# Mixture of experts in float32: gate and up in column blocks of 1024, 1024, 1024, 512 in place of seven of 512

## The reference

```python
def _moe(h, w_router, w_gate, w_up, w_down):       # 8 experts, 2 of them for each token
    ...
    xs = xf[tok_sorted]
    hid = jax.nn.silu(lax.ragged_dot(xs, w_gate, group_sizes)) * lax.ragged_dot(xs, w_up, group_sizes)
    ys = lax.ragged_dot(hid, w_down, group_sizes)
    ys = ys * gates.reshape(-1)[order][:, None].astype(ys.dtype)
    out = jnp.zeros_like(xf).at[tok_sorted].add(ys)
```

## Time and profile before

| | |
|---|---|
| time, median of 3 runs | 2108.22 us (2107.17 to 2116.1) |
| span of the profiled execution | 2110.6 us; nothing of it lies outside the core's span |
| PE busy | 1991.3 us, 94% |
| DVE busy | 1566.7 us, 74% |
| ACT busy | 1266.8 us, 60% |
| moved by DMA | 504.07 MB, 239 GB/s over the span |

### The profile page before, as it was taken

One profiled execution on the slowest core, in us unless ns is written; L12 is line 12 of the kernel. 1 busy time (PEld: TensorE's weight loads), 2 busy tenths in 40 slices (PEclk: granted clock), 3 DMA queues, 4 the chain that ended last, 5 costly groups with the idle time before them and its releaser, 6 DMA issues.

```text
span 2110.6 us, 27963 instructions
## 1 busy us (share of the span) xinstructions
PE 1991.3 (94%) x10196; PEld 1664.4 (79%) x10196; DVE 1566.7 (74%) x1654; ACT 1266.8 (60%) x1469; POOL 373.2 (18%) x165
## 2 busy tenths in 40 slices
PE   6999789999998999988879999999999999999997
PEld 5787678998766899876668878788887888878885
DVE  3336656665677666668769989898998989889896
ACT  3535234433642434465248778787887878788785
POOL 4478463000640300164020000000000000000000
PEclk9899899999999999999989999999999999999999
DMA  8343334555431555542159989899998989999994
GB/s 245 100 160 130 108 112 161 198 181 180 135 96 67 161 193 185 180 126 90 51 199 366 375 319 374 322 371 331 358 377 315 375 321 371 368 323 374 330 365 161
DMA packets 244789, 504.07 MB, mean 239 GB/s; under 512 B 10448, under 2 KB 59216, under 8 KB 244576
## 3 DMA queue, kind: packets, MB, share of 16 engines
q1 hardware_dynamic: 241968, 499.02, 67.0%
q0 software_dynamic: 976, 2.25, 0.5%
q10 hardware_dynamic: 1760, 1.64, 0.2%
HBM read 501.83 MB, written 1.05 MB: 238 GB/s over the span
## 4 chain that ended last, share of the span: by engine, by line
PE 84%; DVE 9%; ACT 3%; issue 2%; DMA 1%; POOL 1%; DVEq 0%; SPq 0%; ACTq 0%
PE bank L565 25%; PE bank L567 24%; PE bank L566 24%; DVE arena L1475 2%; PE bank L994 1%; PE bank L1062 1%; PE bank L1020 1%; DMA arena<-in_w_in 1%; DVE arena L1471 1%; PE bank L626 1%; PE bank L868 1%; POOL w_lo_sb L549 1%; PE bank L763 1%; ACT w_hi_sb L1156 1%; DVE arena L1825 1%
## 5 line engine op out<-in xcount | busy, mean ns | idle before, releaser
L1514 DVE TENSOR_TENSOR w_lo_sb<-arena,w_hi_sb 128x1024 fp32r<-128x1024 f32 x672 | 803.0, 1222 | 92.1 <-ACT w_hi_sb L1136 68.1
L1136 ACT ACTIVATE w_hi_sb<-arena 128x1024 fp32r<-128x1024 f32 x672 | 709.8, 1061 | 185.3 <-PE bank L567 185.3
L565 PE MATMUL bank<-w_hi_sb,left_hi_sb 128*128 128x512 f32 (+1 forms) x1472 | 585.9, 398 | 26.7 <-POOL w_lo_sb L549 9.2
L566 PE MATMUL bank<-w_lo_sb,left_hi_sb 128*128 128x512 f32 (+1 forms) x1472 | 573.0, 389 | 0.0
L567 PE MATMUL bank<-w_hi_sb,left_lo_sb 128*128 128x512 f32 (+1 forms) x1472 | 572.9, 389 | 0.0
L1156 ACT ACTIVATE w_hi_sb<-arena 128x1024 fp32r<-128x1024 f32 (+1 forms) x269 | 279.3, 1051 | 405.9 <-PE bank L567 347.5
L549 POOL TENSOR_TENSOR w_lo_sb<-arena,w_hi_sb 128x1024 fp32r<-128x1024 f32 (+1 forms) x136 | 353.0, 2614 | 694.3 <-ACT w_hi_sb L1156 694.3
L565 PEld LDWEIGHTS bank<-w_hi_sb,left_hi_sb 128*128 128x128 f32 x1472 | 280.8, 191 | 91.7 <-issue 17.3
L567 PEld LDWEIGHTS bank<-w_hi_sb,left_lo_sb 128*128 128x128 f32 x1472 | 280.2, 190 | 58.2
L566 PEld LDWEIGHTS bank<-w_lo_sb,left_hi_sb 128*128 128x128 f32 x1472 | 280.9, 191 | 55.6 <-issue 1.9
L1526 DVE TENSOR_TENSOR w_lo_sb<-arena,w_hi_sb 128x1024 fp32r<-128x1024 f32 x133 | 161.1, 1219 | 132.2 <-ACT w_hi_sb L1156 131.5
(11 more groups left out here) (291 smaller groups left out, 1676.6 us busy)
## 6 DMA issues: line engine op xcount, KB each, us to landing
arena<-in_moe_w_gate SPq DMA_DIRECT2D x112, 1024.0 KB, 7.2
arena<-in_moe_w_up SPq DMA_DIRECT2D x112, 1024.0 KB, 7.3
arena<-in_moe_w_down SPq DMA_DIRECT2D x112, 1024.0 KB, 7.2
arena<-in_w_in SPq DMA_DIRECT2D x46, 1024.0 KB, 5.1
arena<-in_w_ffn_in SPq DMA_DIRECT2D x22, 1024.0 KB, 5.1
arena<-in_w_out SPq DMA_DIRECT2D x12, 1024.0 KB, 5.1
arena<-in_w_ffn_out SPq DMA_DIRECT2D x11, 1024.0 KB, 4.9
arena<-in_dense_w_gate SPq DMA_DIRECT2D x11, 1024.0 KB, 5.4
```

The source lines that it names most:

```text
L565: pe.matmul(out, still[0], moving[0], start=start, stop=False)
L566: pe.matmul(out, still[0], moving[1], start=False, stop=False)
L1136: act.activation(expert_buffer(w_hi_sb, j), expert_piece(j % MOE_SUBS), ACT.Copy) \
L1514: dve.tensor_tensor(expert_buffer(w_lo_sb, j), expert_piece(j % MOE_SUBS), expert_buffer(w_hi_sb, j).bitcast(F32), ALU.subtract) \
```

## The change

Gate and up of an expert are taken in four steps of 1024, 1024, 1024 and 512 columns. A wide step has eight pieces each of gate, up and down. A load of gate or up is two k-tiles of 1024 columns in place of four of 512, so its rows in HBM are 4 KB long and not 2 KB; a piece is one k-tile of 1024 columns, again 1024 words in each partition and six matmuls of 512 columns, which now go to two banks. Gate has banks 0 and 1, up has banks 2 and 3, in every step. `silu`, `turn`, `hidden_hi`, `hidden_lo` and `multiply` of a wide step do two halves of 512 one right behind the other. The counts of loads, pieces, matmuls and all other instructions on data stay as they are. The two loads of the first `down` part are issued in the opposite order, both after the wait for the later of their slots. `place` stands behind `multiply(2)`, as `e_G` does.

```diff
-MOE_STEPS = EXPERT_FF // FF_STEP
+FF_WIDTH = [1024, 1024, 1024, 512]
+FF_AT = [0, 1024, 2048, 3072]
+FF_HALVES = [2, 2, 2, 1]
+FF_HALF_AT = [0, 2, 4, 6]
+MOE_HALVES = EXPERT_FF // FF_STEP
+MOE_STEPS = len(FF_WIDTH)
...
-            return w[:, 4 * second:4 * second + 4, s * FF_STEP:(s + 1) * FF_STEP]
+            k = expert_shape(i)[0]
+            return w[:, k * n:k * n + k, FF_AT[s]:FF_AT[s] + FF_WIDTH[s]]
...
                 for i in range(SLOTS + 2, MOE_LOADS):
-                    freed(it, i - SLOTS)
+                    if expert_loads[i] == ("down", 0, 1):
+                        continue
+                    if expert_loads[i] == ("down", 0, 0):
+                        freed(it, i + 1 - SLOTS)
+                        load(e, i + 1)
+                    else:
+                        freed(it, i - SLOTS)
                     load(e, i)
...
                 def into_hidden(kind, s):
...
+                    pieces = 4 * FF_HALVES[s]
+                    size = KD // pieces
+                    if kind == "gate" and s >= 1:
+                        pe.wait_ge(sem("e_silu_ready"), it * MOE_HALVES + FF_HALF_AT[s])
+                    for i in range(pieces):
+                        w = piece(part_end[kind, s] - pieces + i)
+                        for k in range(size * i, size * i + size):
+                            for half in range(FF_HALVES[s]):
+                                b = gemm_bank[2 * (kind == "up") + half]
+                                mm = three_passes(b[0:CAP, :], (e_hi[:, k, :], e_lo[:, k, :]),
+                                                  [a[:, k % size, half * FF_STEP:(half + 1) * FF_STEP] for a in w],
+                                                  k == 0, k == KD - 1)
                         mm.then_inc(sem("w_used"), 1)
...
                 def silu(s):
                     finished(("gate", s))
-                    act.activation(e_silu[s % 2], gemm_bank[2 * (s % 2)][0:CAP, :], ACT.Silu) \
-                        .then_inc(sem("e_silu_ready"), 1)
+                    if s >= 1:
+                        act.wait_ge(sem("e_hid_ready"), it * MOE_HALVES + FF_HALF_AT[s])
+                    for half in range(FF_HALVES[s]):
+                        act.activation(e_silu[half], gemm_bank[half][0:CAP, :], ACT.Silu) \
+                            .then_inc(sem("e_silu_ready"), 1)
...
                 def multiply(s):
-                    dve.wait_ge(sem("e_silu_ready"), it * MOE_STEPS + s + 1)
+                    dve.wait_ge(sem("e_silu_ready"), it * MOE_HALVES + FF_HALF_AT[s] + FF_HALVES[s])
                     dve.wait_ge(sem("w_used"), it * MOE_SUBS + (USED0 + part_end["up", s]))
-                    dve.tensor_tensor(e_hid[s % 2], e_silu[s % 2], gemm_bank[2 * (s % 2) + 1][0:CAP, :], ALU.mult) \
-                        .then_inc(sem("e_hid_ready"), 1)
+                    for half in range(FF_HALVES[s]):
+                        dve.tensor_tensor(e_hid[half], e_silu[half], gemm_bank[2 + half][0:CAP, :], ALU.mult) \
+                            .then_inc(sem("e_hid_ready"), 1)
...
-                    if s == 4 and more:
+                    if s == 2 and more:
                         place(it + 1, e + 1)
```

More of the change, by code:

```diff
@@ L59 @@
 FF_STEP = 512
-MOE_STEPS = EXPERT_FF // FF_STEP
-MOE_LOADS = 3 * MOE_STEPS * 2
+FF_WIDTH = [1024, 1024, 1024, 512]
[4 more added lines that the diff above has]
+MOE_STEPS = len(FF_WIDTH)
+MOE_LOADS = 3 * MOE_HALVES * 2
 MOE_SUBS = 2 * MOE_LOADS
@@ L428, in build @@
         expert_parts.append(("down", MOE_STEPS - 1))
-        part_end = {part: 4 * n + 4 for n, part in enumerate(expert_parts)}
+        expert_loads, part_end = [], {}
+        for kind, s in expert_parts:
+            expert_loads += [(kind, s, n) for n in range(2 * FF_HALVES[s])]
+            part_end[kind, s] = 2 * len(expert_loads)
         def expert_source(i, e):
-            (kind, s), second = expert_parts[i // 2], i % 2
+            kind, s, n = expert_loads[i]
             if kind == "down":
-                at = s * FF_STEP + second * 2 * P
+                at = FF_AT[s] + n * 2 * P
                 return A["moe_w_down"][e, at:at + 2 * P, :].rearrange("(k p) n -> p k n", p=P)
             w = A[f"moe_w_{kind}"][e].rearrange("(k p) n -> p k n", p=P)
-            return w[:, 4 * second:4 * second + 4, s * FF_STEP:(s + 1) * FF_STEP]
+            k = expert_shape(i)[0]
+            return w[:, k * n:k * n + k, FF_AT[s]:FF_AT[s] + FF_WIDTH[s]]
         def expert_shape(i):
-            return (2, D) if expert_parts[i // 2][0] == "down" else (4, FF_STEP)
+            kind, s, _ = expert_loads[i]
+            return (2, D) if kind == "down" else (SLOT // FF_WIDTH[s], FF_WIDTH[s])
         def expert_piece(j):
@@ L1011, in into_hidden @@
                         mm.then_inc(sem("w_used"), 1)
                 def turn(s):
-                    pe.wait_ge(sem("e_hid_ready"), it * MOE_STEPS + s + 1)
+                    pe.wait_ge(sem("e_hid_ready"), it * MOE_HALVES + FF_HALF_AT[s] + FF_HALVES[s])
                     if s == 0:
                         pe.wait_ge(sem("e_added"), it * 4 + 4)
-                    for i in range(4):
-                        tr = pe.transpose(misc[s % 2][:, i * CAP:(i + 1) * CAP], e_hid[s % 2][:, i * P:(i + 1) * P],
-                                          ident[0:CAP, 0:CAP])
@@ L1022, in turn @@
-                    tr.then_inc(sem("e_hid_turned"), 1)
-                def down(s):
[L1025 to L1029, removed]
+                    for half in range(FF_HALVES[s]):
+                        for i in range(4):
+                            tr = pe.transpose(misc[half][:, i * CAP:(i + 1) * CAP], e_hid[half][:, i * P:(i + 1) * P],
+                                              ident[0:CAP, 0:CAP])
+                        tr.then_inc(sem("e_hid_turned"), 1)
@@ L1030, in down @@
+                def down(s):
+                    pieces = 4 * FF_HALVES[s]
+                    for n in range(pieces):
+                        if n % 4 == 0:
+                            pe.wait_ge(sem("e_hid_split"), it * MOE_HALVES + FF_HALF_AT[s] + n // 4 + 1)
+                        i, hid = n % 4, [tiles(a[n // 4], 4) for a in (hid_hi, hid_lo)]
+                        w = piece(part_end["down", s] - pieces + n)
+                        last = s == MOE_STEPS - 1 and n == pieces - 1
                         for half in range(2):
@@ L1032, in down @@
                                               [a[:, 0, half * 512:(half + 1) * 512] for a in w],
-                                              s == 0 and i == 0, last)
+                                              s == 0 and n == 0, last)
                             if last and half == 0:
@@ L1391, in silu @@
                     finished(("gate", s))
-                    act.activation(e_silu[s % 2], gemm_bank[2 * (s % 2)][0:CAP, :], ACT.Silu) \
-                        .then_inc(sem("e_silu_ready"), 1)
+                    if s >= 1:
[3 more added lines that the diff above has]
+                            .then_inc(sem("e_silu_ready"), 1)
                 def hidden_hi(s):
-                    act.wait_ge(sem("e_hid_turned"), it * MOE_STEPS + s + 1)
-                    act.activation(hid_hi[s % 2], misc_bank[s % 2][:, 0:4 * CAP], ACT.Copy) \
-                        .then_inc(sem("e_hid_hi"), 1)
+                    for half in range(FF_HALVES[s]):
+                        act.wait_ge(sem("e_hid_turned"), it * MOE_HALVES + FF_HALF_AT[s] + half + 1)
+                        act.activation(hid_hi[half], misc_bank[half][:, 0:4 * CAP], ACT.Copy) \
+                            .then_inc(sem("e_hid_hi"), 1)
                 at = BUFFERS
@@ L2019, in multiply @@
                 def multiply(s):
-                    dve.wait_ge(sem("e_silu_ready"), it * MOE_STEPS + s + 1)
+                    dve.wait_ge(sem("e_silu_ready"), it * MOE_HALVES + FF_HALF_AT[s] + FF_HALVES[s])
                     dve.wait_ge(sem("w_used"), it * MOE_SUBS + (USED0 + part_end["up", s]))
-                    dve.tensor_tensor(e_hid[s % 2], e_silu[s % 2], gemm_bank[2 * (s % 2) + 1][0:CAP, :], ALU.mult) \
-                        .then_inc(sem("e_hid_ready"), 1)
+                    for half in range(FF_HALVES[s]):
+                        dve.tensor_tensor(e_hid[half], e_silu[half], gemm_bank[2 + half][0:CAP, :], ALU.mult) \
+                            .then_inc(sem("e_hid_ready"), 1)
                 def hidden_lo(s):
-                    dve.wait_ge(sem("e_hid_hi"), it * MOE_STEPS + s + 1)
-                    dve.tensor_tensor(hid_lo[s % 2], pair_bank[2 + s % 2][:, 0:4 * CAP], hid_hi[s % 2].bitcast(F32),
-                                      ALU.subtract).then_inc(sem("e_hid_split"), 1)
+                    for half in range(FF_HALVES[s]):
+                        dve.wait_ge(sem("e_hid_hi"), it * MOE_HALVES + FF_HALF_AT[s] + half + 1)
+                        dve.tensor_tensor(hid_lo[half], pair_bank[2 + half][:, 0:4 * CAP], hid_hi[half].bitcast(F32),
```

(1 more changed line is left out.)

## The result

| | before | changed |
|---|---|---|
| median, 6 runs each | 2113.87 us | 2126.49 us |
| lowest to highest | 2107.17 to 2117.53 | 2121.0 to 2128.36 |
| ratio | 1 | 1.0066, 95% interval 1.0051 to 1.0081 |
| span of the profiled execution | 2110.6 us | 2120.3 us |

Slower by 0.66%; 0.62% was forecast. The forecast of 2121.2 us stood on the three runs of the kernel before that were known then, with a median of 2108.22; with three more it is 2113.87.

A forecast was written before the change was run, and what follows sets the result against it. The prediction took PE to bound the kernel, losing only what it must wait. First silu 3.9, DVE's block 8.9 and 0.4, less turns 0.2, made 13.0 us on 2108.2: 2121.2 us, range 2110 to 2129.

The forecast's parts named there:

- PE bears 1.41 us: At the first silu of an expert: a piece may be 1.41 us late before PE waits.
- lower bound: The piece behind the one PE waited for was 1.29 us late without a wait, so the limit is at least 1.29.
- upper sum: The total loss if PE bears only 1.29 us of lateness: 15.2 us.
- First silu, 0.10 to 0.59: On ACT, a second silu behind the first raises PE's wait from 0.10 to 0.59 us, +0.49 in each of 8 experts.
- DVE's block, 1.27 in seven experts: Behind multiply of step 2, a second multiply and place make PE wait 1.27 us in seven experts, 0.43 in the last.
- Turns, 0.2 saved: 24 groups of four transposes are joined to others: 0.2 us saved in all, at most 2.4.
- The sum: All terms together: 8 x 0.49 + 7 x 1.27 + 0.43 - 0.2 = 13.0 us slower.
- The other doubled jobs, nothing: Other doubled multiplies, hidden_hi and hidden_lo on ACT and DVE cost nothing; the hidden jobs' cover is 0.3 to 0.4 us.
- Banks and loads, nothing: Gate's reuse of banks that silu reads, and the loads with the later first down load, cost nothing.
- DVE's block was not borne: Rival: DVE's delay behind step 2 is borne, only the silu costs, 2112 us; 15% for 2110 to 2117.
- sped up by larger rows: Rival: 4 KB rows in HBM end a hold-up of PE by arriving packets, 2093 us; chance 4%.
- 0.007 a matmul: The most that DMA could cost PE on each matmul; all of it back would be 28 us.

The follow-up runs named there:

- experiment four: The kernel before with one tiny silu at the head of each expert, so without the table load at the first silu; ratio 0.9995 to the kernel before.
- experiment five: The changed kernel with the tiny silu, a piece between the halves of every doubled job, e_G and place each alone among pieces; ratio 0.9992 to the kernel before.
- Experiment one: The changed kernel with place behind multiply of step 3 instead of step 2; ratio 1.0031 to the kernel before.

## Why the prediction was right, point by point

- **PE bears 1.41 us.** Right within 0.1, at the seven places of the table. The lower bound was read too high: PE was itself 0.10 us behind by the second piece, so what that piece shows to be borne is 1.29 - 0.10 = 1.19. Only the upper sum and the lower end of the cover of the doubled jobs hung on it.
- **First silu, 0.10 to 0.59.** Measured 0.59. The count was off: the description of the kernel before, too, gives every expert a table load at its first silu, but the last one has none there, in either kernel, and no wait. So seven times 0.49 and not eight: 3.4 for 3.9.
- **DVE's block, 1.27 in seven experts.** Measured 1.30, 9.1 for 8.9. In the last expert I said 0.43. There e_G takes 0.64 (2067.31 to 2067.95) and not 0.85. The last expert is the one written out behind the hardware loop; that this is the reason was not tried. The rows of DVE and of PE behind it:

```profile
2064.97 1.23 DVE L1543 TENSOR_TENSOR w_lo_sb<-arena,w_hi_sb 128x1024 fp32r<-128x1024 f32 x1
2066.11 1.28 DVE L2052 TENSOR_TENSOR arena<-arena,bank 128x512 f32<-128x512 f32 x2
2067.31 0.61 DVE L2076 TENSOR_SCALAR arena<-arena 128x128 f32<-128x128 f32 x2
2067.95 1.22 DVE L1543 TENSOR_TENSOR w_lo_sb<-arena,w_hi_sb 128x1024 fp32r<-128x1024 f32 x1
```
```profile
2068.89 0.39 PE L583 MATMUL bank<-w_hi_sb,hid_lo_sb 128*128 128x512 f32 x1
2069.32 0.47 PE L581 MATMUL bank<-w_hi_sb,hid_hi_sb 128*128 128x512 f32 x1
2069.63 0.39 PE L582 MATMUL bank<-w_lo_sb,hid_hi_sb 128*128 128x512 f32 x1
```

  The piece was due at 2064.97 + 1.36 = 2066.33 and began 1.62 later; PE's starts are 0.43 and 0.31 apart: a wait of 0.29 us.
- **Turns, 0.2 saved.** Too little, and it was inside the bound of 2.4. Between the kernels without any wait of PE for a piece, experiments four and five, an expert differs by 0.18 us; between the changed kernel and the one before by 1.66 where the waits make 0.59 + 1.30 - 0.13 = 1.76 (0.13 is what experiment four took out of an expert). That is 0.10 to 0.18 us for three groups joined, 0.8 to 1.4 us in all. The sum left out that PE is slower for a while behind a break in its row of matmuls, as a turn is one: in the trace of experiment four the first six starts behind one are 0.2315 us apart on average, in place of 0.2267, and the next six 0.2276. Experiment five has three such breaks fewer in each expert; with the turns themselves that makes 0.17 of the 0.18.
- **The sum.** 3.4 + 9.1 + 0.3 - 1.0 = 11.8 us for 13.0, and the stage of the experts is 11.8 longer. The spans differ by 9.7, since the stage began 2.0 us earlier in the profile after; over the eight profiles it begins anywhere from 1082.20 to 1088.74, through a part of the program that the change does not touch. The medians differ by 12.6, with 10.8 to 17.1 for the interval, so that this comes closer to 13.0 than the sum by terms does is luck. The absolute time, 2126.49 us, lies above the forecast's own 2118 to 2125, but the kernel before rose by 5.7 as well, from its median of three runs to that of six; the difference is what was forecast. PE was to be idle for 2.1 us of an expert and is for 1.72, as a part of its waits counts as busy. The upper sum of 15.2 left out the 0.2 of the turns.
- **The other doubled jobs, nothing.** Right for the changed kernel. DVE's piece behind two hidden_lo is 0.98 late in the changed kernel, for 0.96 (due at 1385.03 + 1.36 + 1.09 = 1387.48, begun at 1388.46), which leaves about 0.4 of cover. Experiment one used it up.
- **Banks and loads, nothing.** Right. PE never waits for a silu. (ACT is through both silus 1231.60 - 1228.13 = 3.5 us behind that piece, not 3.6.) On the banks the Trainium skill ("Perfetto Trace Analysis", section Optimizing Tensor Performance, Matmuls) has independent groups of matmuls rotate; gate and up still do, and the trace has no wait. Its section DMA Optimizations expects more throughput of larger transfers where a kernel is bound by DMA; this one isn't, and no row of the waits names a load.
- **The rivals.** DVE's block was not borne: it is 9.4 of the 12.8 us of added waiting. PE is not sped up by larger rows: in a stretch without a break 60 starts in a row take 13.60 us in the kernel before (1400.97 to 1414.57) and 13.60 in the changed one (1400.94 to 1414.54), 0.2267 each with rows of 2 KB and of 4 KB. The 0.007 a matmul that the prediction left open came from the rounding of two starts.

## What to carry to other kernels

Where a chain of engines feeds the bound one through a few buffers, ask for each place how late one item may be, read that from the one place where the bound engine just begins to wait, and add up what stands between two items in each feeding queue; busy shares of 90% and 80% say nothing about it. Joining steps into wider ones doubles what stands in a row even though the sum of work stays, so the jobs between items must be spread when steps are widened. The Trainium skill has a hint near this in "Perfetto Trace Analysis", section Optimizing Scalar/DVE Operations: where ScalarE or VectorE aren't saturated but cause bubbles on other engines, breaking up instructions may let work be completed sooner. No run here broke up an instruction; experiment five spread whole ones among the pieces, at a ratio of 0.9992 where the changed kernel beside it had 1.005.

## What the runs showed that I had not expected

- A tiny silu at the head of the loop body took out one of the two table loads of an expert, the one at the first silu. The other stays about where it was, ahead of a split for which ACT waits 2.3 us for PE anyway (2.5 before). ACT is busy for 98.82 us an expert and not 99.69.
- The same two short instructions of DVE with a wait between them cost 0.85 us in an expert of the hardware loop and 0.64 in the last one, outside it.
